# Norm roots and reciprocals on 128x4 token columns, spread over the rows by TensorE, and one wait shortened, in a fused two-block transformer kernel

## The reference

```python
def rms_norm(x, g):
    xf = x.astype(jnp.float32)
    y = xf * lax.rsqrt(jnp.mean(xf * xf, axis=-1, keepdims=True) + EPS)
    return (y * g.astype(jnp.float32)).astype(x.dtype)

        u = rms_norm(h, mix_pre_g[i])
        y = dilated_attention_mixer(u, a_w_in[j], a_w_out[j], cos, sin)
        h = h + rms_norm(y, mix_post_g[i])
        u = rms_norm(h, mem_pre_g[i])
        y = memory_cross_attention(u, rms_norm(mem, mem_kv_g[i]), x_wq[i], x_wkv[i], x_wo[i])
        h = h + rms_norm(y, mem_post_g[i])
        u = rms_norm(h, ffn_pre_g[i])
        y = swiglu_ffn(u, w_gate_up[i], w_down[i])
        h = h + rms_norm(y, ffn_post_g[i])
```

## Time and profile before

| | us |
|---|---|
| median of 3 runs | 3449.95 (3449.45 to 3450.18) |
| profiled execution, its own time | 3454.02 |
| span of the profiled execution, first to last instruction | 3452.2 |
| mean granted TensorE clock | 0.951 |

### The profile page before, as it was taken

One profiled execution on the slowest core, in us unless ns is written; L12 is line 12 of the kernel. 1 busy time (PEld: TensorE's weight loads), 2 busy tenths in 40 slices (PEclk: granted clock), 3 DMA queues, 4 the chain that ended last, 5 costly groups with the idle time before them and its releaser, 6 DMA issues.

```text
span 3452.2 us, 37294 instructions
## 1 busy us (share of the span) xinstructions
PE 3140.3 (91%) x14560; PEld 2444.7 (71%) x14560; DVE 1852.3 (54%) x2608; ACT 1254.1 (36%) x1995; POOL 335.5 (10%) x261
## 2 busy tenths in 40 slices
PE   6898899998898899998998797999889887979997
PEld 4576688886576688885666766888656467668886
DVE  6565544457665544457665546444667644464445
ACT  4544322234544322344444333222333423332222
POOL 2000200013000100012001202000110012020001
PEclk9898999999998999999999999999999989999998
DMA  3110233222110233331112312223211123123322
GB/s 119 43 50 25 74 98 97 94 96 79 43 50 27 77 96 97 98 98 61 54 50 74 110 49 68 97 98 98 74 55 55 37 66 111 44 72 96 95 97 79
DMA packets 72650, 259.07 MB, mean 75 GB/s; under 512 B 7908, under 2 KB 10088, under 8 KB 71976
## 3 DMA queue, kind: packets, MB, share of 16 engines
q1 hardware_dynamic: 71672, 252.73, 22.8%
q0 software_dynamic: 816, 4.13, 0.4%
HBM read 254.73 MB, written 2.10 MB: 74 GB/s over the span
## 4 chain that ended last, share of the span: by engine, by line
PE 55%; issue 29%; DVE 8%; POOLq 3%; ACT 3%; DVEq 2%; POOL 1%; DMA 0%; ACTq 0%; SPq 0%
PE bank L485 40%; POOLq L2489 3%; DVE w_lo L1725 2%; PE bank L968 2%; PE bank L979 1%; PE bank L694 1%; ACT w_hi L1135 1%; PE bank L546 1%; PE bank L989 1%; PE bank L534 1%; PE bank L1005 1%; PE bank L993 1%; PE bank L733 1%; PE bank L512 1%; PE bank L721 1%
## 5 line engine op out<-in xcount | busy, mean ns | idle before, releaser
L485 PE MATMUL bank<-a_hi,w_hi 128*128 128x512 f32 x2040 | 831.3, 408 | 111.0 <-DVE a_lo L1755 47.6
L485 PE MATMUL bank<-a_lo,w_hi 128*128 128x512 f32 x2040 | 804.8, 395 | 0.0
L485 PE MATMUL bank<-a_hi,w_lo 128*128 128x512 f32 x2040 | 804.3, 394 | 0.0
L1725 DVE TENSOR_TENSOR w_lo<-w_raw,w_hi 128x1024 fp32r<-128x1024 f32 (+1 forms) x474 | 621.4, 1312 | 334.3 <-ACT w_hi L1135 332.7
L485 PE MATMUL bank<-b_hi,w_hi 128*128 128x512 f32 (+1 forms) x1688 | 651.3, 386 | 74.2 <-DVE w_lo L1725 38.5
L1135 ACT ACTIVATE w_hi<-w_raw 128x1024 fp32r<-128x1024 f32 (+1 forms) x474 | 493.7, 1043 | 414.2 <-DMA w_raw<-weights 414.2
L485 PE MATMUL bank<-b_lo,w_hi 128*128 128x512 f32 (+1 forms) x1688 | 641.8, 380 | 0.0
L485 PE MATMUL bank<-b_hi,w_lo 128*128 128x512 f32 (+1 forms) x1688 | 640.7, 380 | 0.0
L485 PEld LDWEIGHTS bank<-a_hi,w_hi 128*128 128x128 f32 x2040 | 389.8, 191 | 225.4 <-issue 78.4
L485 PEld LDWEIGHTS bank<-a_lo,w_hi 128*128 128x128 f32 x2040 | 390.5, 191 | 85.8 <-issue 7.9
L485 PEld LDWEIGHTS bank<-a_hi,w_lo 128*128 128x128 f32 x2040 | 389.4, 191 | 84.5
(11 more groups left out here) (274 smaller groups left out, 2998.6 us busy)
## 6 DMA issues: line engine op xcount, KB each, us to landing
w_raw<-weights SPq DMA_DIRECT2D x458, 512.0 KB, 3.4
w_raw<-weights SPq DMA_DIRECT2D x16, 384.0 KB, 3.0
x<-x SPq DMA_DIRECT2D x1, 2048.0 KB, 9.4
mem<-mem POOLq DMA_DIRECT2D x2, 1024.0 KB, 5.3
out<-x SPq DMA_DIRECT2D x8, 256.0 KB, 2.0
mem<-mem SPq DMA_DIRECT2D x1, 1024.0 KB, 14.9
ple<-ple POOLq DMA_DIRECT2D x2, 512.0 KB, 3.8
pos_i<-positions POOLq DMA_DIRECT2D x2, 256.0 KB, 6.7
```

The costliest lines, as they stand in the source:

```text
L485: last = mm(bank[G_BANK[u % 4] if at is None else at][:, 0:cols], w[:, u % SLOTS, ks], t[:, k, 0:cols], start=(k == 0 and n == 0), stop=(k ...
L1725: tt(w_lo[:, u % SLOTS, w], w_raw[:, u % SLOTS, w], f32(w_hi[:, u % SLOTS, w]), ALU.subtract).then_inc(w_lo_ready, 1)
```

## The change

The sum, the root and the reciprocal are now taken on columns of 128 tokens. `sum_squares` makes four matmuls (for 512 tokens) with a block of `sq_sum` as stationary operand and a single column of ones as moving one, so that the 128 tokens of a block come out in the 128 rows of one column of bank 2. ScalarE's root and VectorE's reciprocal work on 128x4 numbers. A new step of TensorE, `spread_root`, makes four matmuls of 128x128: each takes one column of `root`, broadcast, as stationary operand and the identity as moving one, and so writes the reciprocals of 128 tokens along the columns of bank 2, the same in all rows. VectorE then copies the bank (128x512) into `r_x`, `r_post` or `r_mem`. The copy stands in VectorE's queue right behind the reciprocal, and waits there for `r_spread`.

Where the spread stands in TensorE's queue differs: behind the third unit in `ffn1`, `gate`, `xq` and `ffn2`; behind the first half of the third unit in `mix1` and `fused`; right behind the sum in `proj` and at the ends of `out2` and `ffn2`; for the memory, three units behind its sum. The next sum waits for the last copy (`r_copied`) instead of for the root, and ScalarE's root no longer waits for the last reciprocal.

Apart from that, in `fused` the third unit waits for `bank_free` to reach `first` (all units of earlier stages evicted) instead of `u - 1`, which is `first + 1`.

```diff
-        root = place("root", [P, S], F32, at_o + 6 * KB)
+        root = der[:, 58:62]
...
                 pe.wait_ge(sq_added, c.count(sq_added, 8))
                 if c.groups > 0:
-                    pe.wait_ge(root_ready, c.groups)
+                    pe.wait_ge(r_copied, c.groups)
                 c.groups += 1
-                mm(bank[SUM_BANK][:, 0:cols], ones.broadcast_to([P, P]), sq_sum[:, 0:cols],
-                   start=True, stop=True).then_inc(sum_ready, 1)
+                for tb in range(cols // P):
+                    last = mm(bank[SUM_BANK][:, tb:tb + 1], sq_sum[:, qs(tb)], ones, start=True, stop=True)
+                last.then_inc(sum_ready, 1)
+
+            def spread_root(cols=S):
+
+                pe.wait_ge(recip_ready, c.groups)
+                for tb in range(cols // P):
+                    last = mm(bank[SUM_BANK][:, qs(tb)], root[:, tb:tb + 1].broadcast_to([P, P]), ident, start=True, stop=True)
+                last.then_inc(r_spread, 1)
...
@@ mix1 @@
                 sum_squares()
-                halves_of(2)
+                half()
+                if l == 0:
+                    pe.wait_ge(loaded, 48)
+                spread_root()
+                half()
                 if l == 0:
                     memory()
-                halves_of(10)
+                halves_of(6)
+                if l == 0:
+                    spread_root(MEM)
+                halves_of(4)
@@ ffn1, and likewise gate, xq, ffn2 @@
                         sum_squares()
-                    for j in range(2 if first else 0, 8):
+                        unit(a)
+                        spread_root()
+                    for j in range(3 if first else 0, 8):
                         unit(a)
@@ fused @@
                         pe.wait_ge(w_lo_ready, u + 1)
-                        pe.wait_ge(bank_free, u - 1)
+                        pe.wait_ge(bank_free, first if u == first + 2 else u - 1)
...
                 sum_squares()
                 half(0)
+                spread_root()
                 half(1)
                 rotate(0, 0)
...
@@ scalar: root_of_mean @@
                 act.wait_ge(sum_ready, c.count(sum_ready))
-                if c.groups > 0:
-                    act.wait_ge(recip_ready, c.groups)
                 c.groups += 1
-                f(root[:, 0:cols], bank[SUM_BANK][:, 0:cols], ACT.Sqrt, bias=eps, scale=1.0 / D).then_inc(root_ready, 1)
+                n = cols // P
+                f(root[:, 0:n], bank[SUM_BANK][:, 0:n], ACT.Sqrt, bias=eps, scale=1.0 / D).then_inc(root_ready, 1)
@@ vector: recip @@
                 dve.wait_ge(root_ready, c.count(root_ready))
-                dve.reciprocal(dst[:, 0:cols], root[:, 0:cols]).then_inc(recip_ready, 1)
+                dve.reciprocal(root[:, 0:n], root[:, 0:n]).then_inc(recip_ready, 1)
+                dve.wait_ge(r_spread, c.count(r_spread))
+                dve.tensor_copy(dst[:, 0:cols], bank[SUM_BANK][:, 0:cols]).then_inc(r_copied, 1)
                 dve.drain()
```

More of the change, by code:

```diff
@@ L324, in build @@
         act_made, f_ready, y_zero = sem("act_made"), sem("f_ready"), sem("y_zero")
-        sq_ready, sq_added, sum_ready, root_ready, recip_ready = (
-            sem("sq_ready"), sem("sq_added"), sem("sum_ready"), sem("root_ready"), sem("recip_ready"))
+        sq_ready, sq_added, sum_ready, root_ready, recip_ready, r_spread, r_copied = (
+            sem("sq_ready"), sem("sq_added"), sem("sum_ready"), sem("root_ready"), sem("recip_ready"),
+            sem("r_spread"), sem("r_copied"))
         ple_landed, mem_first_landed, mem_landed, pos_landed, dil_landed = sem("ple_landed"), sem("mem_first_landed"), sem("mem_landed"), sem("pos_landed"), sem("dil_landed")
@@ L939, in gate @@
                 sum_squares()
-                for _ in range(6):
+                unit(a)
+                spread_root()
+                for _ in range(5):
                     unit(a)
@@ L1081, in chunk @@
                         sum_squares()
-                    for _ in range(2 if first else 0, 2 * tiles):
+                        unit(a)
+                        spread_root()
+                    for _ in range(3 if first else 0, 2 * tiles):
                         unit(a)
```

1 line of the change is left out of this document (added).

## The result

The change made the kernel slower: 3465.19 us median of 6 runs (3463.16 to 3466.69), against 3449.91 us of before (6 runs, 3449.45 to 3454.26). The ratio is 1.0042 with a 95% interval of 1.0029 to 1.0055, so +15.3 us where +1 was forecast, and above the forecast's range, which ended at 3460.

What follows compares the result with a forecast made beforehand. TensorE, busy 91% of the span, was taken as the bound wherever its work is not waiting. The terms 7.6 + 6.2 + 6.6 + 1.0 - 0.7 - 14.6 - 5.2 gave +0.9 us, 3450.9 us, range 3442 to 3460.

Steps and rivals of the forecast that it cites:

- Prices of sum and spread: At each place, new sum 0.87 us instead of 0.46 and spread 0.85, costing TensorE 1.26 us.
- rival with small matmuls at their own length: Sums and spreads: 16 instructions cost 0.65 us together, about 0.04 each, each place 1.07 cheaper; 3437 us, chance 4%.
- `fused`: Two places: third unit starts at once, rotation 7.5 us after the sum instead of 14.7; -14.6 us together.
- `mix1`: Layer 0 chain shorter, -1.0 us; layer 1 factor later, +0.3; together -0.7.
- `proj`: Two places: second half waits for reciprocal and spread; zero at full clock, +0.5 us each taken, +1.0.
- `kv`: Two places: TensorE waits for reciprocal and spread, starting 3.6 us later; +3.3 each taken, +6.6.
- half-clock rival: Idle TensorE in `kv` and `proj` drops the clock, slowing following work, `post` and starts after `gate`; 3461 us, chance 14%.
- hidden waits: Rival: VectorE slack in `gate` and another limit on `kv` remove their 6.2 and 6.6 us; 3438 us, chance 10%.
- late third unit: Rival: in `fused` the third unit still meets a wait, so the 14.6 shrinks; up to 3465 us, chance 5%.
- `gate`: Two places: VectorE waits for the spread behind the third unit, first eviction 8.3 us after sum; +3.1 each, +6.2.
- `post`: Four places, after `out2` and `ffn2`: sum to factor 3.4 us instead of 5.23; -1.3 each taken, -5.2.
- cheaper six places: `ffn1`, `xq`, `ffn2`, two layers each: TensorE is the bound and pays 1.26 us each, +7.6.

Runs made afterwards that it cites:

- the wait alone: Before with only the third unit's bank wait in `fused` shortened and the norms left as they were: 3437.72 us, ratio 0.9962.
- the kernel with the wait on GpSimd: The hybrid kernel with GpSimd's addition to `x` in `gate` also waiting for VectorE's second split of the same step: 3427.87 us, ratio 0.9939.
- hybrid: Before with shorter `fused` wait; the change's norm only in first `mix1`, `cross` and `ffn2` posts, and `gate` (spread right behind sum): 3431.19 us, ratio 0.9945.

## Why the prediction was wrong, point by point

- **Prices of sum and spread**: right. 0.81 and 0.81 instead of 0.87 and 0.85. A place costs 0.98, not 1.26, because I had credited before's sum with its own 0.46 alone. The matmul behind it was 0.79 long and is 0.49 long now. Counted in the timelines from the sum's start to the third matmul behind it, the old sum kept TensorE 1.31 us and the new one 1.37; the spread adds 0.90. The rival with small matmuls at their own length is out: 0.10 an instruction. With the loads that each carries, the rule of "LDWEIGHTS (loading the stationary operand)" in the Trainium skill's page "TensorE: Matmul & The Clock Gate" (107 ns for 128 columns) comes close at the full clock. At the half clock the spread's eight instructions stand 0.22 apart (1894.95 to 1896.67), twice that figure.
- **`fused`**: right in mechanism and nearly in size, 7.43 against 7.5 from sum to rotation, and -16.1 against -14.6 over both layers; the wait alone has the whole gain.
- **`mix1`**: the -0.6 confirms nothing. 0.5 of it lies ahead of the first sum, where nothing was changed; from there on layer 0 has -0.7 and layer 1 +0.6, against -1.0 and +0.3, in a stage that differs by 3.5 us between two executions of before. The reading that one execution's 4 us carry over was right.
- **`proj`, the step that failed first.** "Zero, if the clock is full; with TensorE idle ahead of it for 6 us it may be at half for a while, +1.3 to +2.2", and then +0.5 was taken, with up to 1.5 back at `ffn1`. The clock was at half, VectorE's copies waited for TensorE, and it cost 2.5 a layer. Nothing came back at `ffn1`: TensorE's gap ahead of it shrank from 12.23 to 4.07 us, and it still began at a granted clock of 0.50. Products in the idle time turned this into -0.4.
- **`kv`, the same step.** The first eviction was put "at 1898.3 if the clock is full (+2.5), and at about 1900 if the first few us are at half of it (+4.2)", and +3.3 was taken, a middle value between two levels, when the wait ahead of the sum had already brought the clock down and the new wait prolonged it. It was at 0.50 through sum, spread and the first 3.5 us of the pair: 5.0 us later at the first eviction, 5.1 and 6.6 over the stage. The half-clock rival had 14% and 3461; since the earlier trace rows already show before's sum at 1.50 instead of 1.02, it should have been given much more. Of the other rivals, the hidden waits are out by `gate`'s and `kv`'s growth, and the late third unit by `fused`.
- **`gate`**: +3.1 was right for the factor (8.27 behind the sum; the second layer shows +3.1 alone). The other 3.1 in layer 0 is the exclusion of VectorE and GpSimd: the shifted chain kept the order in which GpSimd starts first, so that four splits of 1.22 became 2.23. I had read that stage's last eviction and not its splits. That this is what the shift did in `gate` is read from the trace; that the order alone makes the length is shown by the kernel with the wait on GpSimd.
- **`post`**: the mechanism was right and the size mis-set, -0.8 each on average, just short of the half clock's 0.9 where 1.3 was taken: the spread ran at half clock in all four.
- **`cross`**: not in the prediction, since the change has nothing there. The clock fell in it in layer 0, +3.2. As far as is shown this was chance: it fell in before's layer 1 too, and in the wait-only kernel in both.

The four places where the clock fell (`proj` 4.0 over the term, `kv` 5.1, `post` 1.9, `cross` 3.1) make up the 14 us that were missed; the exclusion's 3.1 is made up for by the cheaper six places (1.7) and `fused` (1.5).

## What to carry to other kernels

In this kernel a wait put on TensorE has two prices: its length, and the lower clock behind it. Where TensorE idles some microseconds ahead of a chain on which others wait, reckon what follows at half clock from the start, as one of two levels and not a mean, and ask whether a wait stands ahead of it already; work that nobody reads, measured to fit the gap, gives the difference back. A shorter operation on an engine that was waited for is worth only what its place in the next engine's queue lets through: in `gate` a reciprocal ready 1.5 us after the sum was used at 8.3. And it is worth only what stands ahead of it in its own queue lets through: the same small reciprocal was ready 4.3 us after the sum in `kv` and 7.1 in `proj`. Whether moving it forward there would take TensorE's new waits away was not tried. And where two engines read SBUF at once, read who starts first by a tenth of a microsecond.

## What the runs showed of the hardware that was not expected

- In `gate`, VectorE's `w_lo` (two inputs in SBUF) beside GpSimd's addition: 1.22 us when it starts 0.16 ahead, 2.24 when it starts 0.14 behind. Making GpSimd second throughout took 4.6 us off a stage of 53.0.
- A float32 product of 128 x 128 by 512 columns is two records and takes 0.88 to 0.90 us; the kernel's own products of that shape, in its rounded format, stand 0.23 apart. Twelve records took 5.40.
- The same instructions in the same stage take different times by where the clock falls: `cross` 123.5 or 126.7 us, `mix1` of layer 1 up to `proj`'s sum 334.3 (hybrid) or 337.6 (the same with products elsewhere). A change upstream shifts them, so single stages of sparse TensorE work carry 3 us of luck, and edits worth less need a comparison by stage.
